# Output projection of the second token half, turned to token-major, in the merging stage of a hybrid mixer layer

## The reference

```
y      = sigmoid(mg_m) * (y_m @ w_proj_m) + sigmoid(mg_g) * (y_g @ w_proj_g)     # 1024 x 1024
x      = x + gt1 * (y @ w_out)
h      = rms_norm(x, g_norm2) * (1 + sc2) + sh2
logits = h @ [w_grp | w_rexp]                                                     # 20 columns
```

## Time and profile before

| | us |
|---|---|
| median of 3 runs | 2483.27 (2480.03 to 2490.3) |
| the profiled execution's own time | 2479.71 |
| its span, first to last instruction | 2478.0 |
| TensorE busy in the span | 2170.4 |
| VectorE, ScalarE, GpSimd busy | 1422.3, 1009.3, 853.0 |
| mean granted TensorE clock, share of full speed | 0.935 |

### The profile page before, as it was taken

The page is one execution under the profiler, slowest core; times in us unless marked ns, Lnnn a source line. Parts: engine busy times, 40 slices in busy tenths (PEclk is TensorE's granted clock), DMA queues, the critical chain, the costliest instruction groups (busy, mean ns, idle before and its releaser), DMA issues. The chain is left out here.

```text
span 2478.0 us, 26742 instructions
## 1 busy us (share of the span) xinstructions
PE 2170.4 (88%) x10286; PEld 1758.7 (71%) x10286; DVE 1422.3 (57%) x1711; ACT 1009.3 (41%) x1263; POOL 853.0 (34%) x630
## 2 busy tenths in 40 slices
PE   6979979996599995799999959999759999999992
PEld 1268867884487884688888847788558778887882
DVE  0535542101433332788988635444258899998993
ACT  1412210111144444355555444432216666766762
POOL 5300000000256654366776621220113344443541
PEclk9989999998699997799999969999859999999996
DMA  7633324213355665243444376563349966469535
GB/s 276 247 75 94 97 74 182 85 47 113 112 177 156 179 179 185 77 133 117 122 124 122 91 235 204 165 221 119 108 181 347 371 215 195 115 182 340 154 60 161
DMA packets 262890, 398.75 MB, mean 161 GB/s; under 512 B 27046, under 2 KB 186918, under 8 KB 255980
## 3 DMA queue, kind: packets, MB, share of 16 engines
q1 hardware_dynamic: 233068, 243.90, 30.9%
q0 software_dynamic: 27968, 147.89, 18.9%
q10 hardware_dynamic: 1728, 5.25, 0.6%
HBM read 401.68 MB, written 88.67 MB: 198 GB/s over the span
## 5 line engine op out<-in xcount | busy, mean ns | idle before, releaser
L2587 DVE TENSOR_TENSOR ex_w_lo<-ex_raw,ex_w_hi 128x2048 fp32r<-128x2048 f32 x186 | 415.9, 2284 | 37.9 <-ACT ex_w_hi L2449 37.9
L2449 ACT ACTIVATE ex_w_hi<-ex_raw 128x2048 fp32r<-128x2048 f32 x182 | 337.7, 1909 | 168.6 <-DMA ex_raw<-in_w_up_dram,rt_w_rows 87.0
L682 POOL DMA_DIRECT2D vals<-rows_stage x40 | 21.9, 547 | 440.4 <-ACT rows_stage L674 440.4
L2319 POOL DMA_INDIRECT ex_raw<-in_w_up_dram,rt_w_rows x60 | 75.8, 1263 | 138.4 <-DVE ex_w_lo L2587 132.9
L1544 PEld LDWEIGHTS gl_lv_ps<-gl_q_level,gl_k_level 128*128 128x128 f32 x896 | 108.1, 194 | 11.3 <-issue 8.5
L2319 POOL DMA_INDIRECT ex_raw<-in_w_down_dram,rt_w_rows x30 | 52.0, 1734 | 183.3 <-DVE ex_w_lo L2587 176.9
L2012 DVE TENSOR_TENSOR mo_w_lo<-mo_w,mo_w_hi 128x1024 fp32r<-128x1024 f32 x48 | 59.8, 1246 | 94.2 <-ACT mo_w_hi L1909 94.2
L1544 PE MATMUL gl_lv_ps<-gl_q_level,gl_k_level 128*128 128x64 f32 x896 | 110.5, 276 | 3.5 <-DVE gl_scores L1674 1.7
L908 PE MATMUL gl_u_ps<-half_hi,gl_u_w_hi 128*128 128x512 f32 x256 | 107.9, 421 | 4.4 <-ACT gl_u_exp L926 4.4
L674 ACT ACTIVATE rows_stage<-rows_ps 128x512 f32<-128x512 f32 x40 | 23.9, 599 | 212.3 <-PE rows_ps L651 212.3
L908 PE MATMUL ml_u_ps<-half_hi,ml_u_w_hi 128*128 128x512 f32 x256 | 104.9, 410 | 6.2 <-ACT ml_u_exp L926 6.2
(11 more groups left out here) (401 smaller groups left out, 6070.9 us busy)
## 6 DMA issues: line engine op xcount, KB each, us to landing
fr_w<-in_w_mod_dram SPq DMA_DIRECT2D x12, 2048.0 KB, 9.9
ml_u_w<-in_w_in_dram SPq DMA_DIRECT2D x32, 512.0 KB
gl_u_w<-in_w_in_dram SPq DMA_DIRECT2D x32, 512.0 KB, 5.1
vals<-rows_stage POOLq DMA_DIRECT2D x40, 256.0 KB, 2.3
ml_v<-vals SPq DMA_DIRECT2D x20, 512.0 KB, 4.0
gl_v<-vals SPq DMA_DIRECT2D x20, 512.0 KB, 3.4
qk_w<-in_w_in_dram SPq DMA_DIRECT2D x16, 512.0 KB, 4.8
rows_w<-in_w_in_dram SPq DMA_DIRECT2D x8, 1024.0 KB, 7.4
```

The source lines that it names most:

```text
L2319: pool.indirect_dma_start(out=raw[:, q, :], out_offset=None, in_=sources[q], in_offset=bass.IndirectOffsetOnAxis(ap=w_rows[:, q, b:b + 1], ...
L2449: act.activation(hi[:, q, h], raw[:, q, h], ACT.Copy).then_inc(hi_done[q], 1)
L2587: dve.tensor_tensor(lo[:, q, at], raw[:, q, at], hi[:, q, at].bitcast(F32), ALU.subtract)\
```

## The change

In the second half, group 2 (units 40 to 47, `LAST` to `NU - 1`) becomes `out_rows`. The output block is now a row tile of 128 tokens by 512 channels: the block of `y` stands in the array and the weights move. Units 40 to 43 are channels 0 to 511 of the tiles 4 to 7, units 44 to 47 channels 512 to 1023. The number and form of the matmuls is the same. The weights are loaded in eight pieces of two depth blocks by 512 columns and split into the buffers that held the branches (`br_hi`, `br_lo`). All four pieces of the first 512 channels must be there for the first of these units, so pieces and units share the two slots in a new order (`ORDER`), with two splits in each of the steps 36, 37 and 38.

VectorE takes a unit out (`take_out`): it multiplies by a row of `gt1` that is the same in all partitions (loaded into the former gate buffer `og`), and adds the product into `x`, which is loaded into `hin` for all four tiles (`load_rows`, at step 25 of SP's list, behind the loads of that step). Turning by `turn_x`, the scaling on ScalarE, and `load_x` of the tiles 4 to 7 go away for this half. A tile is ready after its second unit, so norm, shift and router of tile 4 to 6 start while later units run: VectorE calls `normed` in the loop; TensorE turns tile 4 ahead of unit 47; the rest follows after it. The router's results of four tiles lie side by side in one bank and are copied once per half.

```diff
+        LAST = NU - KD
+        ORDER = list(range(LAST - 2)) + [LAST, LAST - 2, LAST + 1, LAST - 1] + list(range(LAST + 2, NU))
+        SPLIT_IN = {u: [u + 1] for u in range(LAST - 4)}
+        SPLIT_IN.update({LAST - 4 + i: places for i, places in enumerate(
+            ([LAST - 3, LAST - 2], [LAST - 1, LAST], [LAST + 1, LAST + 2], [LAST + 3]))})
+        SPLIT_IN.update({LAST + i: [LAST + 4 + i] for i in range(4)})
+        LOAD_IN = {u + 1: [p + 2 for p in places if p + 2 < NU] for u, places in SPLIT_IN.items()}
 ...
+            def load_rows():
+                sp.wait_ge(gated, 4 * KD)
+                sp.dma_start(flat(og[:, :, :]), m.mod_rows[:, 0:D]).then_inc(gt_row_loaded, 16)
+                sp.wait_ge(turned, 4 * KD)
+                for t in range(TH):
+                    sp.dma_start(hin[:, t, :], w["x"][0][(TH + t) * P:(TH + t + 1) * P, :]).then_inc(in_loaded[t], 16)
 ...
+            def take_out(u):
 ...
+                dve.wait_ge(made, u + 1)
+                dve.tensor_tensor(part, ps[:, u % 3, :], flat(og[:, :, :])[:, cols], ALU.mult).then_inc(out_left, 1)
+                dve.wait_ge(out_left, n + 1)
+                dve.wait_ge(in_loaded[t], 16 * 5)
+                last = dve.tensor_tensor(hin[:, t, cols], hin[:, t, cols], part, ALU.add)
 ...
             for u in range(NU):
-                if u:
+                if u > LAST:
+                    take_out(u - 1)
+                elif u:
                     leave(u - 1)
-                if u + 1 < NU:
-                    weight_lo(u + 1)
+                if u - 1 >= LAST + 4:
+                    normed(u - 1 - LAST - 4 + TH)
+                for place in SPLIT_IN.get(u, ()):
+                    weight_lo(place)
 ...
+            def out_rows(u):
 ...
+                out, at = ps[:, u % 3, :], slice(t * P, (t + 1) * P)
+                for k in range(KD):
+                    if t == 0 and k % 2 == 0:
+                        pe.wait_ge(wl_done, PLACE[LAST + 4 * c + k // 2] + 1)
+                    if u == LAST:
+                        pe.wait_ge(yl_done, KD + k + 1)
+                    pe.matmul(out, y_hi[:, k, at], br_hi[:, c, k, :], start=(k == 0), stop=False)
+                    pe.matmul(out, y_hi[:, k, at], br_lo[:, c, k, :], start=False, stop=False)
+                    last = pe.matmul(out, y_lo[:, k, at], br_hi[:, c, k, :], start=False, stop=(k == KD - 1))
 ...
-            for at in range(TH + 5):
-                tile_steps(at, TH)
+            for u in range(LAST, NU):
+                out_rows(u)
+                if u == NU - 2:
+                    turn_h(TH)
+            router(TH)
+            for i in range(TH + 1, NL):
+                turn_h(i)
+                router(i)
```

More of the change, by code:

```diff
@@ L1865, in _ @@
             for u in range(NU):
-                if u and u + 2 < NU:
-                    load_w(u + 2)
+                for place in LOAD_IN.get(u, ()):
+                    load_w(place)
                 if u and u + 1 < NU:
@@ L1967, in _ @@
                 tile_steps(u - AFTER_O, 0)
-            leave(NU - 1)
-            for at in range(TH + 4):
-                tile_steps(at, TH)
+            tile_norm(TH)
+            tile_norm(TH + 1)
+            tile_turned(TH)
+            tile_norm(TH + 2)
+            tile_norm(TH + 3)
+            for i in range(TH + 1, NL):
+                tile_turned(i)
         @block.gpsimd
@@ L2008, in gate_branch, with weight_lo @@
                                          in1=og[:, g % OG, :], op0=ALU.mult, op1=ALU.mult).then_inc(gated, 1)
[L2010 to L2013, removed]
+            def weight_lo(place):
+                u = ORDER[place]
+                dve.wait_ge(wh_done, place + 1)
+                if u < LAST:
+                    high, low = flat(w_hi[:, u % 2, :, :]), flat(w_lo[:, u % 2, :, :])
+                else:
+                    high, low = piece_of(br_hi, u), piece_of(br_lo, u)
+                dve.tensor_tensor(low, flat(w_raw[:, place % 2, :, :]), high.bitcast(F32), ALU.subtract)\
+                    .then_inc(wl_done, 1)
+            def take_out(u):
+                c, t = out_piece(u)
+                n = u - LAST
+                cols = slice(c * HF, (c + 1) * HF)
+                part = br[:, n % 2, :]
+                if n == 0:
+                    dve.wait_ge(gt_row_loaded, 16)
+                    dve.wait_ge(b_lo, 4 * KD)
+                elif n >= 2:
+                    dve.wait_ge(row_half, n - 1)
+                dve.wait_ge(made, u + 1)
[3 more added lines that the diff above has]
+                last = dve.tensor_tensor(hin[:, t, cols], hin[:, t, cols], part, ALU.add)
+                last.then_inc(row_half, 1)
+                if c:
+                    dve.wait_ge(row_half, n + 1)
+                    dve.sem_inc(x1_done, 1)
             def leave(u):
@@ L2085, in _ @@
                 tile_steps(u - AFTER_O, 0)
-            for at in range(TH + 5):
-                tile_steps(at, TH)
-            dve.wait_ge(logits, NL)
+            take_out(NU - 1)
+            normed(NL - 1)
+            keep_logits(TH)
+            dve.wait_ge(logits, 2)
         @block.tensor
@@ L2151, in router @@
                 pe.wait_ge(h_t, i + 1)
-                if i:
-                    pe.wait_ge(logits, i)
-                else:
+                if i == TH:
+                    pe.wait_ge(logits, 1)
+                elif i == 0:
                     pe.wait_ge(wr_loaded, 32)
                 for k in range(KD):
-                    last = pe.matmul(ps[:, 7, 0:GROUPS + EXPERTS], h2t[:, k, :], wr[:, k, :],
+                    last = pe.matmul(ps[:, 7, i % TH * RL:(i % TH + 1) * RL], h2t[:, k, :], wr[:, k, :],
                                      start=(k == 0), stop=(k == KD - 1))
@@ L2169, in _ @@
                 turn(g)
-            for u in range(NU):
+            for u in range(LAST):
                 unit(u)
```

95 lines of the change are left out of this document (61 added, 34 removed).

## The result

| | before | after |
|---|---|---|
| median of 7 runs each, side by side, us | 2484.5 (2479.52 to 2490.3) | 2469.02 (2462.32 to 2473.55) |
| ratio, with its 95% interval | | 0.9938 (0.9922 to 0.9954) |
| profiled execution | 2479.71 | 2469.02 |
| last turn of `mo_in` to the end of the last logits | 201.78 | 181.31 |
| of it the tail behind the last projection matmul | 47.40 | 22.05 |

Faster by 15.5 us, 0.6% (11.4 to 19.4 us by the interval), inside the range and 8 us above the forecast. The line from the last turn of `mo_in` to the last logits is the part of the merging stage that the change touches, measured from the start of a turn that both kernels have: there 20.5 us are gone, where 21.8 were forecast.

The account below looks back on a forecast made before the run. TensorE bounds the second half's units; behind them no engine does, but a 47.4 us chain handed between engines. Terms of -26.4, +1.0, +0.2, +1.2 and +2.2 sum to -21.8 us, from 2483.27 to 2461, range 2450 to 2471.

Parts of the forecast that it names:

- Tail, -26.4: Behind the last projection matmul: the chain to the last logits shrinks from 47.4 to 21 us, clock falling at about E + 4.
- Rival A: In the tail: the clock holds, 14.5 us in place of 21, giving 2455 us; chance 0.15.
- Loads at step 25, +2.2: First half: five more loads, 2.6 MB, delay `x` of tile 2, so TensorE waits about 2.2 us before turning tile 3.
- Supply of weights, +0.2: Steps 36 to 38: two splits each, two slots, loads landing after 3.4 us; unit 39 starts 0.2 us late.
- `y`'s last block, +1.2: Unit 40: VectorE splits the last block of `y` about 1.2 us later, so TensorE waits 1.2 us more.
- Turn of tile 4, +1.0: On TensorE in front of unit 47: tile 4's eight transposes take 1.0 us, with no wait for the tile.
- The matmuls, 0: Units 40 to 47: 192 matmuls of 512 columns with operands exchanged, neither gain nor loss taken.
- Sum, -21.8: Whole change: -26.4 + 1.0 + 0.2 + 1.2 + 2.2 us, giving 2461 us; forecast's chance 0.62.
- three signs of being wrong: Projection loop over 50 us, weights waited for by DMA in it, or a tail over 25 us.
- Rival B: Units 38 to 40: weight loads come late and DMA sets the pace, +12 us in place of 1.4, 2472; chance 0.17.
- C: Token-major loop: gaps in units 38 to 43 pull the clock down, another 45 us, 2506, slower than before; chance 0.03.
- D: Tail: no gain, as norm and router do not get beside the matmuls; tail would have to last 43 us; chance 0.03.

Follow-up runs that it names:

- Run 5: Changed kernel plus short 20-column products that nobody reads in the tail's gaps on TensorE; tail 22.09 us.
- run 6: Changed kernel plus 512-column products that nobody reads in the tail's gaps on TensorE; tail 15.68 us, stage 175.20 us.
- experiment 2: Changed kernel with the five loads at step 25 put off to steps 31 to 35, one transfer a step; 2469.36 us, ratio 0.9948.
- run 9: Changed kernel with later loads, more work inside units 46 and 47, shift on VectorE, earlier last `y` split, dense fillers; 2451.4 us against 2482.1, ratio 0.9877.
- run 3: Changed kernel with the second and third product of a depth block exchanged in the channel-major units; ratio 0.9942, stage 181.61 us.
- run 1: Changed kernel and the one before profiled again without edit; stage 181.14 and 183.21 us with the change, 202.50 and 202.37 before.
- run 7: Changed kernel with tile 4's turn in unit 46, its router and tile 5's turn in unit 47, copy 5 earlier; tail 14.09 us, stage 176.80.

## Why the prediction was right

Unit starts are counted from the last turn of `mo_in`.

- **Tail, -26.4: measured -25.4.** Router 5 starts 5.48 us behind the last projection matmul where 4.5 were forecast, as ScalarE's copy of tile 5 stands behind the statistics of tile 7 (named in the forecast), and those came 1.2 us late by the slow add (not named: the sum had 0.69 for it, from a row where it ran alone). The fall of the clock, taken half way between two ends at 4 us behind the last matmul, came at about 5.8 (0.81 over 1786 to 1789 is 1.86 us at full clock). Router 5, itself late, ran nearly all at half clock all the same (3.30), so that the tail came out within 1.1 us is in part luck. Rival A's price was right (6.1 measured, 6.5 forecast) and its condition was not met.
- **The clock.** The forecast weighed the Trainium skill, page "TensorE: Matmul & The Clock Gate", section "HAM oscillation — how this bites in real kernels", against a busy window at 0.50 and took the row. Run 5 bears that out: without a gap, the clock fell to 0.50 all the same; run 6 kept 1.00 with dense products in the same places. The page's account by idle gaps does not cover this tail, and the measurement decides.
- **Loads at step 25, +2.2: 2.4** (unit 37 starts at 94.92 after 92.51). The named wait at the turn of tile 3 is 1.62 of it, and experiment 2 shows that the loads make it; the later one grew from 2.35 to 2.97, where the forecast had it unchanged, and experiment 2 leaves open why.
- **Supply of weights, +0.2: 1.7** (unit 40 starts 4.15 late, less the 2.4). This is the term that was mis-sized. The walk through the two slots took a landing of 3.4 us, from loads issued one at a time, 5.6 us apart. Of the eight loads from 1705 to 1735 here six are issued in pairs, 1.1 to 1.5 us apart, and the eight took 3.7 to 5.0, with a median of 4.2. ScalarE waited 1.22, 0.22, 0.30 and 0.40 for them, and with no reserve in the slots TensorE got it: waits of 0.58 and 0.68. Two of ScalarE's waits, in its timeline:

```profile
1721.57 1.06 ACT L1952 ACTIVATE mo_w_hi<-mo_w 128x1024 fp32r<-128x1024 f32 x1 [1.22 <-DMA mo_w<-in_w_proj_g_dram]
...
1729.53 1.06 ACT L1952 ACTIVATE mo_branch_hi<-mo_w 128x1024 fp32r<-128x1024 f32 x1 [0.40 <-DMA mo_w<-in_w_out_dram]
```

In run 9 the loads of this stretch took 3.3 to 4.5, median 3.9, and the three units lost 0.8. That the pairs are what made the loads slower is not shown: no run issued them apart.
- **`y`'s last block, +1.2: 0.9** (unit 40 lasts 6.72 where units of its kind are 5.44 apart; before, 5.95 and 5.58). **Turn of tile 4, +1.0: 0.8** (units 46 to 47 6.23 apart, not 5.44).
- **The matmuls, 0: -1.1**, by the closer spacing of run 3. The forecast took nothing here because engine and shape stay the same; that this makes up for most of the mis-sized supply is luck.
- **Sum, -21.8: -20.5** (the terms above give -20.7). None of the three signs of being wrong came: the loop of units 40 to 47 took 45.87 us, the tail 22.05, and the late pieces were waited for at units 38 and 39, ahead of the loop. Rival B's mechanism, late weight pieces, is there at 1.7 us of its 12; C is refuted by clock 1.00 in units 40 to 47, D by the tail.
- **Outside the stage, 0: about +5 by the medians** (-15.5 against -20.5). Two or three of them are the experts' stage (+3.6 in the first pair of profiles, +2.5 in the pair of run 1). The scans ahead of the stage came out 4.2 longer in the changed kernel's first profile, with the same code; single profiles differ there by more: the kernel before took 783.4, 791.2 and 783.4 us in its three, from the first matmul of the mLSTM mixer to the last of the other. What is left of the gap is less than the interval of the medians.

## What to carry to other kernels

When work is moved beside a loop, price each of its operations with the neighbour that it will then have, and not by a row where it ran alone: VectorE's add took two to three times as long beside GpSimd's shift, and moving the shift to VectorE was the cheaper place. A handed-on chain at the end of a stage pays twice, in hand-overs and in the clock: put as many links as possible inside the dense loop, and what can't go there may be worth some dense products that nobody reads. A supply with two slots and no reserve should be summed with the slowest landings seen, and not with a median from a kernel that had one load under way at a time: here up to 5.0 us in place of 3.4, and 1.7 us lost in place of 0.2.

## What had not been expected of the hardware

- In this kernel 512-column matmuls come every 0.227 us with the activations in the array and the weights moving, and every 0.232 with these exchanged, at clock 1.00 both; the order of the products makes no difference.
- With TensorE busy 3.00 of 3.00 us by 20-column products, the granted clock went from 1.00 to 0.56 to 0.50; with 512-column ones in their places it stayed at 1.00.
- An add of two SBUF operands on VectorE takes 0.69 us alone and 1.40 to 2.10 when it starts beside GpSimd's shift (1.21 and 1.40 in run 7), and ends 0.54 or 0.55 behind the shift each time; the shift of 128 x 1024 takes 2.35 to 2.40 on GpSimd and 1.23 on VectorE.
